# Gated product's sigmoids and roots left in PSUM, its squares on ScalarE

## The chip, the cores and the metric

The kernel runs on one core of one Trainium2 chip. The metric is the device time of one execution in microseconds. TensorE is called PE here, VectorE DVE, ScalarE ACT, GpSimd POOL and SyncE SP, as in the profile.

## The reference

The reference computes two blocks of a language model in fp32 over 1024 tokens (with 16 meta tokens before them) and a width of 1024. The first block mixes two branches, differential attention and a state-space model (SSM), each 512 wide. What the change touches is the end of the SSM branch. Its output `y` goes through

```python
y = jax.nn.gelu(y, approximate=False)
y = y * jax.nn.sigmoid(jnp.einsum('blc,cd->bld', y, w_glu[l]) + b_glu[l])
y = rms_norm(y, ssm_out_g[l]).astype(h.dtype)
mix = jnp.einsum('blc,cd->bld', jnp.concatenate([o, y], axis=-1), w_out[l])
```

where `o` is the attention's output. Behind it come a norm, a feed-forward of width 2816 and a second block with retention, a recurrent mixer and a feed-forward of its own.

## The kernel before, in words

Each engine has its own program, written as Python generators that are stepped in one common order. The 1024 tokens are worked in two halves of 512. A matrix product in nearly full fp32 is made of three products of split operands (high by high, low by high, high by low). Weights come in units of 128x1024, in a stream of fixed order (`ORDER`), into six slots. SP loads a unit into a slot when PE has released the unit six before it; POOL then splits it, first the high part (line 560), then the low part (line 562). PE's products with these units follow.

The gated product (`glu(h)` in the programs of ACT, PE and DVE) has features on the partitions: four tiles of 128x512, index `m`. It has six steps, and between them the stepping puts other work of the same engine.

- Steps 1 and 2: ACT issues 32 small loads of `y_raw`, applies Gelu in place and copies the high part `yh`. DVE makes the low part `yl`.
- Step 3: PE makes the products with the gate's weights, 48 matmuls (line 1752), into four PSUM banks: 2, 3, 0, 1 in half 0, and 4 to 7 in half 1.
- Step 4: ACT makes four sigmoids from PSUM into the SBUF tile `sig` (line 983) and loads the table of exp and ln. DVE multiplies `y_raw` by `sig` and squares it into `ysq`, tile by tile (lines 2572 and 2575). In half 0 it waits before the square for the second weight unit's products.
- Step 5: PE sums the squares over the 512 features with a matrix of ones (line 1759), in plain fp32, into the tile's first bank.
- Step 6: ACT makes the root `rinv` by ln and exp (lines 989 and 990) into SBUF. DVE scales `y_raw` by it and by the gain (line 2581), ACT copies the high part into `act_hi` (line 994), DVE makes the low part `act_lo` (line 2586).

ACT's operations have line 675 in the profile, DVE's `tt` line 2249 and `stt` line 2256, since helpers issue them. ACT's table loads have line 670.

What surrounds the two halves differs. In half 0 the steps 3 to 6 lie among the last steps of half 0's attention. ACT has that attention's last root (o_sq) between steps 4 and 6 and its last output copy ahead of step 6; DVE has the normalization o_n. After step 6, ACT stores the last query/key tile (line 808) and, when `glu_lo` has come, loads queries, keys and values of half 1's attention (lines 889 to 896). PE makes the first eight of the output product's 32 pieces (`mix_product(0)`, line 1854; one piece is six matmuls), then waits for the keys (line 1664). Those pieces use banks 0 to 3; bank 2 holds the sums of squares.

In half 1 the gated product is interleaved with half 0's feed-forward: behind step 3 stand 4 pieces of gate 20 (line 1813, six matmuls each), behind step 4 the 4 pieces of up 20, behind step 5 the 8 pieces of gate 21 and up 21, behind step 6 the last 16 pieces of the down product (line 1842). On DVE that puts the product `ff_f` (line 2930), its low part `ffh_lo` (line 2934) and the additions to `acc_dense` behind the steps; on ACT the silu `ff_f`, which needs another table, and the copy `ffh_hi`. A down piece waits until DVE has added the piece two before it. Then comes the norm of the feed-forward (`residual_half(0)`).

Of the kernel before, what the change touches and what calls it, by code (L numbers as in the profile page):

```python
# [7 lines left out]
F32, F32R, BF16 = mybir.dt.float32, mybir.dt.float32r, mybir.dt.bfloat16  # L8
ACT = mybir.ActivationFunctionType
ALU = mybir.AluOpType  # L10
X_AXIS = mybir.AxisListType.X
MUL, ADD, SUB = ALU.mult, ALU.add, ALU.subtract
# [51 lines left out]
class Tally:  # L64
# [11 lines left out]
    def give(self, ins, sem):  # L76

        self.eng.wait_ge(sem, self.post(ins, sem))
# [7 lines left out]
def build(nc, t):  # L86
# [179 lines left out]
    def glu_tiles(h):  # L266
        at = (ARENA, AT_MIX)[h]
        tiles_at = [place(f"y_raw_{h}", [P, 4, OCT, BANK // OCT], F32, at)]
        for n, (name, dt) in enumerate((("yh", F32R), ("yl", F32R), ("ysq", F32), ("sig", F32))):
            tiles_at.append(place(f"{name}_{h}", [P, 4, BANK], dt, at + 8192 * (n + 1 if h or n < 2 else 2 * n - 3)))  # L270
        tiles_at.append(place(f"rinv_{h}", [P, BANK], F32, at + (40960 if h else 16384)))
        return tiles_at

    glu_at = [glu_tiles(0), glu_tiles(1)]
# [383 lines left out]
    def _(act):  # L658
# [9 lines left out]
        def table_for(func):  # L668
            if loaded[0] != SETS[func]:
                act.preload_act_table_set(SETS[func])  # L670
                loaded[0] = SETS[func]

        def fn(out, in_, func, **kw):
            assert func not in SETS or loaded[0] == SETS[func]
            return act.activation(out, in_, func, **kw)  # L675
# [280 lines left out]
                    yield  # L956

        def glu(h):
            y_raw, yh, yl, ysq, sig, rinv = glu_at[h]
            if h == 0:  # L960
                spills_landed(0, 1)
            y_view = t["y_scratch"].rearrange("(t h) g c -> h t g c", h=SG)
            c0 = (META + BANK * h) // OCT
            for m in range(4):
                for j in range(8):
                    act.dma_start(y_raw[SG * j:SG * j + SG, m], y_view[:, :, 8 * m + j, c0:c0 + BANK // OCT]).then_inc(y_landed, 16)  # L966
            yield
            table_for(ACT.Gelu)
            act.wait_ge(y_landed, 16 * 32 * (h + 1))
            whole = lambda a, m: a[:, m].rearrange("p t c -> p (t c)")  # L970
            for m in range(4):
                give(fn(whole(y_raw, m), whole(y_raw, m), ACT.Gelu), act_step)
            for m in range(4):
                give(fn(yh[:, m], whole(y_raw, m), ACT.Copy), y_hi)
            yield
            yield
            table_for(ACT.Sigmoid)
            for m in range(4):
                if m % 2:
                    act.wait_ge(unit_done, AT[h, U_GLU + m // 2] + 1)  # L980
                else:
                    take(glu_psum)
                give(fn(sig[:, m], ps[:, glu_bank(h, m), :], ACT.Sigmoid, bias=glu_vec[:, m:m + 1]), glu_sig)
            table_for(ACT.Exp)
            yield
            yield
            table_for(ACT.Ln)
            take(glu_sum)
            give(fn(rinv[:, :], ps[:, glu_bank(h, 0), :], ACT.Ln, bias=eps_col, scale=1.0 / (4 * P)), act_step)
            give(fn(rinv[:, :], rinv[:, :], ACT.Exp, scale=-0.5), glu_root)  # L990
            cols = slice(META + BANK * h, META + BANK * h + BANK)
            for m in range(4):
                act.wait_ge(glu_prod, 4 * (2 * h + 1) + m + 1)
                give(fn(act_hi[:, 4 + m, cols].rearrange("p (c t) -> p t c", t=OCT), y_raw[:, m], ACT.Copy), glu_hi)
            yield
# [488 lines left out]
    def _(pe):  # L1484
# [250 lines left out]
                    yield  # L1735

        def glu(h):
            y_raw, yh, yl, ysq, sig, rinv = glu_at[h]
            yield
            yield  # L1740
            pe.wait_ge(y_lo, 4 * (h + 1))
            pe.wait_ge(*((o_lo, HEAD_UNITS * 2) if h else (y_kept, 2 * TB)))
            for m in range(4):
                pos = AT[h, U_GLU + m // 2]
                pe.wait_ge(w_ready, pos + 1)
                if h == 0 and m == 2:
                    pe.wait_ge(proj_kept, len(PROJ) + len(FAR))
                    pe.wait_ge(rope_done, ROPES + 8)
                for k in range(4):
                    w0 = BANK * (m % 2) + P * k  # L1750
                    for w, a in PASSES:
                        mm = pe.matmul(ps[:, glu_bank(h, m), :], ws[w][:, pos % SLOTS, w0:w0 + P], (yh, yl)[a][:, k, :],
                                       start=(k, w, a) == (0, 0, 0), stop=(k, w, a) == (3, 1, 0))
                post(mm, unit_done if m % 2 else glu_psum)
            yield
            yield
            for m in range(4):
                pe.wait_ge(glu_sq, 4 * h + m + 1)
                mm = pe.matmul(ps[:, glu_bank(h, 0), :], ones[:, :], ysq[:, m, :], start=m == 0, stop=m == 3)
            post(mm, glu_sum)  # L1760
            yield
            yield

        def mix_product(h):
            if h:
                pe.wait_ge(down_added, 2 * HALF * (FT // 2))
            else:
                pe.wait_ge(glu_sig, 4)
            for j, uu, k in OUT_ORDER:
                if (j, k) == (0, 0):  # L1770
                    pe.wait_ge(*((o_lo, HEAD_UNITS * (h + 1)) if uu < 2 else (glu_lo, 4 * (h + 1))))
                if j and uu == 0:
                    pe.wait_ge(mix_kept, 2 * HALF * h + k + 1)
                if (h, j, uu, k) == (0, 0, 0, 2):
                    pe.wait_ge(glu_root, 1)
                token_product(AT[h, U_OUT + 4 * j + uu], k, uu, acts, tok_cols(HALF * h + k), (0, 3, 0), mix_psum)
                yield

# [124 lines left out]
        def residual_half(h):  # L1903
            if h:
                pe.wait_ge(rw_norm, nth("norm", "out", NT - 1))
                pe.wait_ge(rw_act, nth("act", "y", NT - 1))
                pe.wait_ge(rw_dve, nth("dve", "st0", NT - 1))
            else:
                pe.wait_ge(glu_root, 2)
            tiles = tiles_of(2)[HALF * h:HALF * h + HALF]  # L1910
            for step in range(NORM_STEPS):
                if 1 <= step <= HALF:
                    g = tiles[step - 1][0]
                    pe.wait_ge(xn_ready, g + 1)
                    pe.wait_ge(act_ready, g - 1)
                    for k in range(KT):
                        mm = pe.transpose(ps[:, 4 + 2 * (g % 2) + k // 4, P * (k % 4):P * (k % 4) + P], xn_mix[:, g % 2, P * k:P * k + P], ident[:, :])
                    post(mm, turned)
                yield
            pe.wait_ge(act_ready, NT + 1 + HALF * (h + 1))  # L1920
# [323 lines left out]
    def _(dve):  # L2244
# [3 lines left out]
        def tt(out, a, b, op, signal=dve_step):  # L2248
            give(dve.tensor_tensor(out, a, b, op), signal)  # L2249
# [4 lines left out]
        def stt(out, a, s, b, op0, op1, signal=dve_step):  # L2254

            give(dve.scalar_tensor_tensor(out=out, in0=a, scalar=s, in1=b, op0=op0, op1=op1), signal)  # L2256
# [301 lines left out]
                yield  # L2558

        def glu(h):  # L2560
            y_raw, yh, yl, ysq, sig, rinv = glu_at[h]
            yield
            whole = lambda a, m: a[:, m].rearrange("p t c -> p (t c)")
            for m in range(4):
                take(y_hi)
                tt(yl[:, m], whole(y_raw, m), yh[:, m].bitcast(F32), SUB, y_lo)
            yield
            yield
            for m in range(4):
                take(glu_sig)  # L2570
                y = whole(y_raw, m)
                tt(y, y, sig[:, m], MUL, glu_prod)
                if h == 0:
                    dve.wait_ge(unit_done, AT[0, U_GLU + 1] + 1)
                tt(ysq[:, m], y, y, MUL, glu_sq)
            yield
            yield
            take(glu_root)
            for m in range(4):
                y = whole(y_raw, m)  # L2580
                stt(y, y, glu_vec[:, 4 + m:5 + m], rinv[:, :], MUL, MUL, glu_prod)
            cols = slice(META + BANK * h, META + BANK * h + BANK)
            for m in range(4):
                take(glu_hi)
                turned = lambda a: a[:, 4 + m, cols].rearrange("p (c t) -> p t c", t=OCT)
                tt(turned(act_lo), y_raw[:, m], turned(act_hi).bitcast(F32), SUB, glu_lo)
            yield
# [599 lines left out]
```

## Time and profile before

| | us |
|---|---|
| median of 3 runs | 3511.36 |
| lowest and highest | 3508.91, 3519.01 |
| profiled execution, its own time | 3521.95 |
| its span | 3520.0 |
| PE busy, of the span | 3117.6 |
| DVE busy | 1741.5 |
| ACT busy | 849.4 |
| POOL busy | 1975.2 |

All times in the trace are microseconds from the start of the span. The profiled execution is one of its own; none of the three runs was as long. A granted clock of 1.00 is PE's 2.4 GHz, 0.50 is 1.2 GHz. Matmuls overlap, so the time of one matmul in a row is longer than its distance to the next; for a train of matmuls the chain of waits gives the distance.

### The profile page before, as it was taken

The page shows a single profiled execution, that of the slowest core. Times are in us where ns is not written, and L with a number is a line of the kernel's source. Part 1 is how long each engine was busy: PE and PEld are TensorE (multiplying, and loading weights), DVE is VectorE, ACT ScalarE, POOL GpSimd, SP SyncE. Part 2 cuts the span into 40 slices and gives each one's busy share as a digit, 9 for nine tenths or more (in the row PEclk, how much of TensorE's full clock was granted, in tenths as well). Part 3 has the DMA queues.
Part 4 walks back from the last instruction along what each step waited for, and adds up shares of the span by engine and source line. Part 5 has one row for each costly group of instructions (what it writes and reads, how often), then busy time and mean ns, then how long its engine had stood idle before and what let it go on. Part 6 is the DMA issues. An engine that isn't in the chain of part 4 may idle for free.

```text
span 3520.0 us, 47870 instructions
## 1 busy us (share of the span) xinstructions
PE 3117.6 (89%) x19536; PEld 2399.0 (68%) x19536; DVE 1741.5 (49%) x2368; ACT 849.4 (24%) x1583; POOL 1975.2 (56%) x1076
## 2 busy tenths in 40 slices
PE   6997878799998749989999989988999988899997
PEld 4765546577776547767777767776777766688875
DVE  5844543444442641666655654376556564322233
ACT  3111122322221232122323223122222331200012
POOL 5710322454554545746666656665766674577873
PEclk9887888899999879999999999999999999899998
DMA  4343322222222324322222243432222222322231
GB/s 154 108 124 96 102 70 93 90 72 84 72 66 78 120 96 139 116 83 82 74 80 85 67 140 122 138 97 77 80 76 70 91 76 67 126 96 93 93 102 54
DMA packets 158027, 329.99 MB, mean 94 GB/s; under 512 B 34960, under 2 KB 74064, under 8 KB 157808
## 3 DMA queue, kind: packets, MB, share of 16 engines
q1 hardware_dynamic: 58752, 213.94, 19.2%
q10 hardware_dynamic: 99056, 112.99, 10.2%
q8 instruction: 155, 2.54, 0.3%
q14 instruction: 64, 0.52, 0.0%
HBM read 281.89 MB, written 44.97 MB: 93 GB/s over the span
## 4 chain that ended last, share of the span: by engine, by line
PE 72%; DVE 18%; ACT 3%; ACTq 3%; DMA 2%; issue 2%; POOL 0%; DVEq 0%
PE ps L1813 30%; PE ps L1854 12%; PE ps L1842 12%; PE ps L1664 2%; DVE acc_dense L2249 1%; DVE ffh_lo L2934 1%; DVE added L2249 1%; DVE cab_s L2249 1%; DVE act_lo L2249 1%; PE ps L1545 1%; PE ps L1585 1%; PE ps L2048 1%; ACTq L966 1%; DVE xn_dense L2256 1%; PE ps L1575 1%
## 5 line engine op out<-in xcount | busy, mean ns | idle before, releaser
L560 POOL TENSOR_TENSOR w_hi<-w_raw,ones 128x1024 fp32r<-128x1024 f32 x408 | 798.9, 1958 | 1268.5 <-DMA w_raw<-weights 1265.2
L562 POOL TENSOR_TENSOR w_lo<-w_raw,w_hi 128x1024 fp32r<-128x1024 f32 x408 | 1010.1, 2476 | 32.0
L1813 PE MATMUL ps<-act_hi,w_hi 128*128 128x512 f32 x1696 | 703.6, 415 | 13.6 <-ACT qk_raw L675 8.1
L1813 PE MATMUL ps<-act_lo,w_hi 128*128 128x512 f32 x1696 | 677.6, 400 | 0.0
L1813 PE MATMUL ps<-act_hi,w_lo 128*128 128x512 f32 x1696 | 673.4, 397 | 0.0
L1813 PEld LDWEIGHTS ps<-act_hi,w_hi 128*128 128x128 f32 x1696 | 323.6, 191 | 108.4 <-issue 16.5
L1813 PEld LDWEIGHTS ps<-act_hi,w_lo 128*128 128x128 f32 x1696 | 323.2, 191 | 74.9
L1813 PEld LDWEIGHTS ps<-act_lo,w_hi 128*128 128x128 f32 x1696 | 323.6, 191 | 67.1 <-issue 2.0
L2249 DVE TENSOR_TENSOR acc_dense<-acc_dense,ps 128x512 f32<-128x512 f32 x352 | 241.9, 687 | 232.2 <-PE ps L1842 173.3
L1842 PE MATMUL ps<-w_hi,ffh_hi 128*128 128x512 f32 x704 | 295.0, 419 | 56.3 <-DVE acc_dense L2249 55.0
L1842 PE MATMUL ps<-w_lo,ffh_hi 128*128 128x512 f32 x704 | 280.8, 399 | 0.0
L1842 PE MATMUL ps<-w_hi,ffh_lo 128*128 128x512 f32 x704 | 280.6, 399 | 0.0
L1854 PE MATMUL ps<-w_hi,act_hi 128*128 128x512 f32 x640 | 264.0, 412 | 14.8 <-issue 6.5
L1854 PE MATMUL ps<-w_hi,act_lo 128*128 128x512 f32 x640 | 258.8, 404 | 0.0
L1854 PE MATMUL ps<-w_lo,act_hi 128*128 128x512 f32 x640 | 257.5, 402 | 0.0
L2930 DVE TENSOR_TENSOR ff_f<-ff_f,ps 128x512 f32<-128x512 f32 x88 | 60.5, 688 | 374.5 <-PE ps L1813 373.7
L1842 PEld LDWEIGHTS ps<-w_hi,ffh_hi 128*128 128x128 f32 x704 | 135.5, 192 | 99.5 <-DVE acc_dense L2249 65.9
L670 ACT ACT_TABLE_LOAD x141 | 180.9, 1283 | 38.9 <-issue 29.4
L2337 DVE TENSOR_REDUCE small<-ps 128x1 f32<-128x144 f32 (+7 forms) x64 | 49.6, 774 | 223.4 <-PE ps L1666 223.2
L1854 PEld LDWEIGHTS ps<-w_hi,act_hi 128*128 128x128 f32 x640 | 125.1, 196 | 48.8 <-issue 12.3
L1842 PEld LDWEIGHTS ps<-w_lo,ffh_hi 128*128 128x128 f32 x704 | 135.4, 192 | 30.6
L1842 PEld LDWEIGHTS ps<-w_hi,ffh_lo 128*128 128x128 f32 x704 | 136.2, 193 | 25.3
(374 smaller groups left out, 4471.9 us busy)
## 6 DMA issues: line engine op xcount, KB each, us to landing
w_raw<-weights SPq DMA_DIRECT2D x408, 512.0 KB, 3.5
rw<-rw_t ACTq DMA_DIRECT2D x24, 256.0 KB, 2.5
rw<-lora_t ACTq DMA_DIRECT2D x24, 256.0 KB, 2.0
row<-x ACTq DMA_DIRECT2D x8, 512.0 KB, 3.8
row_dense<-x ACTq DMA_DIRECT2D x8, 512.0 KB, 4.1
res<-row_dense ACTq DMA_DIRECT2D x8, 512.0 KB, 2.6
row_mix<-res ACTq DMA_DIRECT2D x8, 512.0 KB, 7.6
res<-row_mix ACTq DMA_DIRECT2D x8, 512.0 KB, 2.8
```

Of the source, the lines that this page charges most:

```text
L560: pool.tensor_tensor(w_hi[:, s], raw, ones[:, 0:1].to_broadcast([P, 1024]), MUL).then_inc(w_hi_made, 1)
L562: pool.tensor_tensor(w_lo[:, s], raw, w_hi[:, s].bitcast(F32), SUB).then_inc(w_ready, 1)
L670: act.preload_act_table_set(SETS[func])
L966: act.dma_start(y_raw[SG * j:SG * j + SG, m], y_view[:, :, 8 * m + j, c0:c0 + BANK // OCT]).then_inc(y_landed, 16)
L1545: mm = pe.matmul(ps[:, n % 2, 0:c1 - c0], ws[w][:, pos % SLOTS, P * k:P * k + P], acts[a][:, k, c0:c1], start=(k, w, a) == (0, 0, 0), stop ...
L1664: mm = pe.matmul(out[:, c:c + w], q, k[:, META + c:META + c + w], start=True, stop=True)
L1813: mm = pe.matmul(out, ws[w][:, s, P * k:P * k + P], acts[a][:, k, x], start=(k, w, a) == (0, 0, 0), stop=(k, w, a) == (KT - 1, 1, 0))
L1842: mm = pe.matmul(ps[:, 2 + n % 2, :], ffh[a][:, m % 4, P * k:P * k + P], ws[w][:, s, BANK * j:BANK * j + BANK], start=(m % 2, w, a) == (0, ...
L1854: mm = pe.matmul(ps[:, kinds[2] + k, :], source[a][:, 2 * uu + kk, x], ws[w][:, pos % SLOTS, BANK * kk:BANK * kk + BANK], start=(uu, kk, w ...
L2249: give(dve.tensor_tensor(out, a, b, op), signal)
L2337: give(dve.tensor_reduce(small[:, col:col + 1], score_rows(h, u, br), X_AXIS, ALU.max, negate=True), s_max)
L2930: give(dve.tensor_tensor(ff_f[:, m % 2], ff_f[:, m % 2], ps[:, 1, :], MUL), ff_prod)
```

## The change

`sig` and `rinv` are no longer tiles in SBUF. The sigmoids go back into the PSUM banks that they are read from, and so does the root, in both of its steps. DVE reads both from PSUM. The squares are made by ACT, all four behind the table load of step 4, each after a wait for DVE's product; DVE's squares and its wait for the second unit are gone. Where PE waited for sigmoids or a root before it wrote to these banks again, it now waits for DVE's products: `glu_prod` counts eight in each half, four gated products and four scalings.

```diff
     def glu_tiles(h):
...
-        for n, (name, dt) in enumerate((("yh", F32R), ("yl", F32R), ("ysq", F32), ("sig", F32))):
+        for n, (name, dt) in enumerate((("yh", F32R), ("yl", F32R), ("ysq", F32))):
...
-        tiles_at.append(place(f"rinv_{h}", [P, BANK], F32, at + (40960 if h else 16384)))
...
 (ACT)   def glu(h):
...
-                give(fn(sig[:, m], ps[:, glu_bank(h, m), :], ACT.Sigmoid, bias=glu_vec[:, m:m + 1]), glu_sig)
+                give(fn(ps[:, glu_bank(h, m), :], ps[:, glu_bank(h, m), :], ACT.Sigmoid, bias=glu_vec[:, m:m + 1]), glu_sig)
             table_for(ACT.Exp)
+            for m in range(4):
+                act.wait_ge(glu_prod, 8 * h + m + 1)
+                give(fn(ysq[:, m], whole(y_raw, m), ACT.Square), glu_sq)
...
-            give(fn(rinv[:, :], ps[:, glu_bank(h, 0), :], ACT.Ln, bias=eps_col, scale=1.0 / (4 * P)), act_step)
-            give(fn(rinv[:, :], rinv[:, :], ACT.Exp, scale=-0.5), glu_root)
+            root = ps[:, glu_bank(h, 0), :]
+            give(fn(root, root, ACT.Ln, bias=eps_col, scale=1.0 / (4 * P)), act_step)
+            give(fn(root, root, ACT.Exp, scale=-0.5), glu_root)
...
 (PE)    def mix_product(h):
...
-                pe.wait_ge(glu_sig, 4)
+                pe.wait_ge(glu_prod, 4)
...
                 if (h, j, uu, k) == (0, 0, 0, 2):
-                    pe.wait_ge(glu_root, 1)
+                    pe.wait_ge(glu_prod, 8)
...
 (PE)    def residual_half(h):
...
-                pe.wait_ge(glu_root, 2)
+                pe.wait_ge(glu_prod, 16)
...
 (DVE)   def glu(h):
...
-                tt(y, y, sig[:, m], MUL, glu_prod)
-                if h == 0:
-                    dve.wait_ge(unit_done, AT[0, U_GLU + 1] + 1)
-                tt(ysq[:, m], y, y, MUL, glu_sq)
+                tt(y, y, ps[:, glu_bank(h, m), :], MUL, glu_prod)
...
-                stt(y, y, glu_vec[:, 4 + m:5 + m], rinv[:, :], MUL, MUL, glu_prod)
+                stt(y, y, glu_vec[:, 4 + m:5 + m], ps[:, glu_bank(h, 0), :], MUL, MUL, glu_prod)
```

## Rows read from the trace of the kernel before

**Rows 1.** The page: busy time by engine, and the chain that ended last.

```profile
PE 3117.6 (89%) x19536; PEld 2399.0 (68%) x19536; DVE 1741.5 (49%) x2368; ACT 849.4 (24%) x1583; POOL 1975.2 (56%) x1076
...
PE 72%; DVE 18%; ACT 3%; ACTq 3%; DMA 2%; issue 2%; POOL 0%; DVEq 0%
```

**Rows 2.** Chain in order of time, half 0: start, us, what.

```profile
540.97 2.40 DVE y_raw L2249
...
549.25 5.49 PE ps L1759 x6
...
555.35 0.70 ACT rinv L675
```

**Rows 3.** Chain in order of time, half 1.

```profile
1140.38 5.60 PE ps L1813 x24
...
1148.70 1.72 DVE y_raw L2249
...
1161.29 3.78 PE ps L1759 x4
1165.07 11.77 PE ps L1813 x48
...
1177.68 2.24 DVE y_raw L2256
...
1190.26 0.70 DVE acc_dense L2249
```

**Rows 4.** Tiles y_raw, acc_dense, rw_t: duration ns min/median/max, first and last start.

```profile
L2249 DVE TENSOR_TENSOR y_raw<-y_raw,sig x8: 691/2018/2717, 541.0 to 1161.3; 128x512 f32<-128x512 f32 x8
L2249 DVE TENSOR_TENSOR ysq<-y_raw x8: 691/693/2711, 543.4 to 1162.0; 128x512 f32<-128x512 f32 x8
L2256 DVE SCALAR_TENSOR_TENSOR y_raw<-y_raw,small,rinv x8: 751/752/2724, 556.8 to 1183.0; 128x512 f32<-128x512 f32 x8
...
L2249 DVE TENSOR_TENSOR act_lo<-y_raw,act_hi x8: 1078/1141/1290, 560.0 to 1189.1; 128x512 fp32r<-128x512 f32 x8
...
L2249 DVE TENSOR_TENSOR acc_dense<-acc_dense,ps x352: 686/687/692, 765.5 to 3427.4; 128x512 f32<-128x512 f32 x176
...
L2256 DVE SCALAR_TENSOR_TENSOR rw_t<-ps,rw_vec_s,rw_t x28: 749/749/751, 1329.5 to 2242.8; 128x511 f32<-128x511 f32 x28
```

**Rows 5.** Timeline of POOL, 1174 to 1186: start, us, engine, line, what.

```profile
1174.99 1.89 POOL L560 TENSOR_TENSOR w_hi<-w_raw,ones 128x1024 fp32r<-128x1024 f32 x1 [15.03 <-DMA w_raw<-weights]
1176.97 2.40 POOL L562 TENSOR_TENSOR w_lo<-w_raw,w_hi 128x1024 fp32r<-128x1024 f32 x1
1180.41 2.04 POOL L560 TENSOR_TENSOR w_hi<-w_raw,ones 128x1024 fp32r<-128x1024 f32 x1 [1.05 <-DMA w_raw<-weights]
1182.53 2.68 POOL L562 TENSOR_TENSOR w_lo<-w_raw,w_hi 128x1024 fp32r<-128x1024 f32 x1
```

**Rows 6.** Timeline of DVE, half 1, the low parts.

```profile
1185.79 4.43 DVE L2249 TENSOR_TENSOR act_lo<-y_raw,act_hi 128x512 fp32r<-128x512 f32 x4
```

**Rows 7.** Timelines of ACT, the table loads behind the sigmoids.

```profile
541.25 1.28 ACT L670 ACT_TABLE_LOAD   x1
...
1150.78 1.28 ACT L670 ACT_TABLE_LOAD   x1
```

**Rows 8.** Groups of ACT by form: busy us, mean ns, idle before.

```profile
L675 ACT ACTIVATE yh<-y_raw 128x512 fp32r<-128x512 f32 x8 | 5.1, 632 | 0.3
```

**Rows 9.** Windows: us, busy time by engine, granted clock, DMA share.

```profile
544.00:545.00 1.00, 0.86 (x2) 0.30 (x2) 0.97 (x2) 0.00 (x0) 1.00 (x1) 1.00 0.00 0
...
546.00:547.00 1.00, 0.00 (x0) 0.00 (x0) 0.96 (x2) 0.00 (x0) 1.00 (x1) 0.50 0.00 0
```

**Rows 10.** Waits of PE, 526 to 582: us, times, longest.

```profile
PE ps L1664 <- DMA k_pair<-qk_scratch: 8.0, 1, 8.0
```

**Rows 11.** Timeline of PE, start of the output product.

```profile
555.81 0.47 PE L1854 MATMUL ps<-w_hi,act_hi 128*128 128x512 f32 x1 [0.87 <-issue]
```

**Rows 12.** Tile acc_dense, the residual additions: min/median/max ns.

```profile
L2249 DVE TENSOR_TENSOR row_mix<-row_mix,acc_dense x8: 1224/2012/3253, 1217.1 to 2105.1; 128x1024 f32<-128x1024 f32 x8
```

More of the change, by code:

```diff
@@ L958, in glu @@
         def glu(h):
-            y_raw, yh, yl, ysq, sig, rinv = glu_at[h]
+            y_raw, yh, yl, ysq = glu_at[h]
             if h == 0:
@@ L1737, in glu @@
         def glu(h):
-            y_raw, yh, yl, ysq, sig, rinv = glu_at[h]
+            y_raw, yh, yl, ysq = glu_at[h]
             yield
@@ L2560, in glu @@
         def glu(h):
-            y_raw, yh, yl, ysq, sig, rinv = glu_at[h]
+            y_raw, yh, yl, ysq = glu_at[h]
             yield
```

## The prediction, made before the changed kernel ran

> **What bounds the kernel now.** The page comes first: TensorE (PE) is busy for 89% of the span, and 72% of the chain that ended last is PE's, 18% VectorE's (DVE) [rows 1]. So time is to be had only where the chain leaves PE. The chain by time shows two such places in the changed code. In half 0 it runs on DVE from 540.97, the first product of y and sigmoid, to the last sums of squares, and reaches the logarithm of the root at 555.35 [rows 2]. In half 1 it is on DVE from 1148.70 to 1161.29, on PE to 1176.84, and on DVE again from 1177.68 to 1190.95, when PE goes on with the feed-forward [rows 3]. The end of the half-0 stage leads into the load of K, for which PE waits 8.0 us [rows 10].
>
> The forms of the tiles say why DVE is slow there. Its instructions with both tensors in SBUF take 0.69 or 0.75 us at best and 2.7 us at worst: y times sigmoid has a median of 2.02 us. The same operations with one operand in PSUM take 0.686 to 0.692 us in all 352 cases, and 0.749 to 0.751 us in all 28 [rows 4]. The long ones lie beside GpSimd's (POOL's) splits of weights, which take about 1.9 and 2.4 us alone and 2.04 and 2.68 us where DVE is in the way [rows 5]. The two exclude each other when DVE reads two SBUF tensors, and a PSUM operand takes DVE out of it.
>
> **The change, part by part, half 0.** Products: each goes from up to 2.7 us to 0.69 us. Four with 0.03 us between, from 540.97, end at 543.87. DVE's four squares are gone. Squares: ACT (ScalarE) does them at 0.63 us, the size of its copy between SBUF tiles [rows 8], after the table load that ends at 542.53 [rows 7]; the first product is done by 541.7. They end at 543.2, 543.9, 544.5 and 545.2. Behind them on ACT wait the attention's last root (three small instructions, done by about 546.2) and DVE's normalization behind it, just in time for PE's turn of the output. Sums: the last three took 5.49 us at the lower clock (0.50 granted) [rows 2, 9], 1.83 us each, so 0.92 at the full clock. Before, the clock was still full in 544 to 545 and at 0.50 in 546 to 547, after some three microseconds in which PE had done little but the first sum [rows 9]. Now the four sums follow each other from 543.25, so I take the full clock: 3.66 us, end 546.9. The old tail from the sums to the logarithm is 555.35 less 554.74, 0.61 us; the new logarithm starts at 547.5. **Gain 7.85 us.**
>
> What follows keeps its length: root, scalings from PSUM at 0.75 us as now, ACT's copies, the stores, the loads. The new wait of the output product's third tile, for all four scalings instead of the root, stops PE. PE starts that product at 555.81 [rows 11]; two tiles of six matmuls (5.60/24 each [rows 3]) last 2.8 us, to 558.6; the scalings end 3.1 us after the root, at 559.9. PE stands 1.3 us, with everything queued behind it. That costs nothing, since PE then waits 8.0 us for K anyway [rows 10]; 6.7 us of the cover are left. Without that cover it would cost the 1.3 us. The weight slot of this product also comes free 1.3 us later; the next split then lies behind DVE's low parts, not among them. The residual's new wait, for 16 products instead of root 2, is over before PE comes to it, more than 20 us later.
>
> **Half 1.** The sigmoids start as now, the products end at 1151.6. ACT's table load ends at 1152.06 [rows 7], so the first square is there at 1152.7 and the last at 1154.7. Behind them on ACT wait the feed-forward's high part and a table load; DVE's low part needs them, PE not before the products 18 us later. The sums run from 1152.75 to 1156.4; before, PE went on from them at 1165.07. The next 48 matmuls took 11.77 us, partly at the lower clock; at twice 5.60 for 24 they take 11.2 [rows 3]. They end at 1167.6 instead of 1176.84: 9.2 us.
>
> Then the DVE stretch, counted from its first scaling (1177.68 before). Before, scalings and low parts took 12.55 us, the low parts 4.43 of them without a meeting [rows 6]. Four scalings from PSUM now take 3.1 us, 5 us less. But POOL's next split follows PE's release of a slot, so it keeps its distance: 2.73 us after the first scaling (1180.41) [rows 5]. The low parts read two SBUF tensors (y and its high part) and come at 3.1 us, into that split. They wait until 4.6; the first (1.08 us) ends at 5.7; POOL's second instruction, 2.4 us, gets in next, to 8.1; the other three end at 11.4. What the scalings win comes back to 1.2 us. **Gain 9.2 + 1.2 = 10.4 us.**
>
> Bounds of what no row shows. ACT writing PSUM: at the lower end nothing changes (0.69 us); at the far end twice that. It would add 0.7 us for the last sigmoid and 1.3 for the root in half 0, and 2.8 for four sigmoids in half 1: 4.8 us. I take the lower end, because DVE's own accesses to PSUM are no slower [rows 4]. A product reading PSUM is bounded by 0.687 and by 2.7; 380 rows lie at the lower end [rows 4]. The removed tiles and the removed wait of DVE for the second unit (long done) cost and give nothing.
>
> Squares moved to ACT cost 0.63 us against 0.69 on DVE [rows 8, 4]. The Trainium skill, page "ScalarE: Activation LUTs", section "Rules for kernel authors", says that such plain arithmetic belongs on VectorE; by the rows of fp32 here the move would lose nothing per instruction. The page "VectorE: DVE Perf Modes", section on the TRN2 errata, gives a PSUM source 62 cycles more than an SBUF source; as an estimate that is 0.065 us, and for some eight instructions on the path 0.5 us less gain. The rows show no such difference.
>
> **Sum:** 7.85 + 10.4 = 18.25 us. The profiled execution took 3521.95 us (span 3520.0), so it would become 3503.7. It lies 10.6 us above the median of the three runs (3511.36, 3508.91 to 3519.01), a difference spread over a program whose other parts the change leaves alone, so I take the sum off the median: **3493.1 us**.
>
> **Rivals.**
> *The meeting does not move.* If POOL's split comes later than the low parts, these keep 4.43 us and the DVE stretch wins 4.95 instead of 1.2: 3489.3 us. For it: only 0.4 us decide (2.73 against 3.1). Against it: if DVE goes first, POOL's work falls between its instructions all the same. Chance 0.13.
> *The clock stays low.* If the sums in both halves run at 0.50, each set takes 3.66 us more and the matmuls behind them 0.6: 7.9 us of the gain are gone, 3501.0 us. For it: the fall before 546 came soon after short work, and short work precedes the sums now too. Against it: the gaps that preceded the fall are filled. Chance 0.17.
> *PSUM writes are slow, or small losses add up,* so that under 10.5 us are left: about 3502 to 3509. Chance 0.12.
> *Lost meetings behind the stage: slower.* The norms after 1213 read two SBUF tensors, 1024 wide, and lie on the chain. The residual additions take 1.22 us at least, 2.01 in the median and 3.25 at most [rows 12]: a lost meeting with POOL costs up to 2.0 us. Between 1213 and 1320 there are 24 instructions of this kind. Nine new losses use up the gain, and from fifteen on the kernel is slower by more than can be told: 18.25 less 30 is 11.7 us more, 3523 us. Against it: many of the 24 are lost already, and POOL's splits and DVE's norms both follow PE's releases and shift together. Chance 0.03.
>
> **How the numbers follow.** The forecast case has 0.55, at 3493, with 4 us each way for the runs' own spread. A measurement of this kernel tells some 0.3%, 10.5 us, from no change. The range takes in the case without the meeting below (3489, less 5 for the spread) and the low clock above (3501, plus 4): 3484 to 3505. Faster: the forecast and the first rival, nearly all, plus some of the low-clock case, which lies at the edge: 0.79. Same: the rest of that and the small losses, 0.17. Slower: 0.04.
>
> **What would show it.** Products and scalings at 0.69 and 0.75 us, all sixteen; squares on ACT at 0.63; sums in one train, 3.4 to 3.7 us, at a granted clock of 1.00; the half-0 logarithm 6.5 us after DVE's first product instead of 14.4; PE's stop of 1.3 us before the third output tile, with the wait for K shorter by as much; in half 1 the low parts at 2 us or more for the first two, and PE resuming about 10.4 us sooner, net of the shift from half 0. I am wrong if products from PSUM are long beside POOL, if the sums have 1.7 us each, if the K wait grows by what the stage lost, or if the norms after the stage take longer than before.

## The result, and the profile after

| us | median | lowest, highest | runs | ratio to before |
|---|---|---|---|---|
| before, measured beside it | 3519.2 | 3508.91, 3522.39 | 6 | |
| changed kernel | 3493.7 | 3486.75, 3499.16 | 6 | 0.9933 [0.9915, 0.9952] |
| its profiled execution | 3495.0 | | 1 | (span 3492.8) |

The ratio gives 0.67% less time, about 24 us, with an interval from 17 to 30 us; the two medians are 25.5 us apart. So the changed kernel is faster, clear of the noise. The prediction was 3493.1 us.

Runs of one and the same kernel lie 13 us apart in the table above (kernel before), and up to 34 us in a longer series (act_squares, below). Spans differ too: a second trace of the kernel before has 3506.9 us where the first has 3520.0. So two spans cannot show terms of a few microseconds. What can be compared is a short stretch between two named instructions, and the readings of terms below are such stretches.

The chain by time of the changed kernel shows half 0. Columns as in [rows 2].

```profile
530.84 1.21 ACT L669
...
532.14 0.64 ACT ysq L674
...
532.82 3.70 PE ps L1762 x8
...
537.03 0.67 ACT ps L674
...
544.30 2.21 DMA qk_scratch<-qk_raw
...
548.25 5.79 DMA k_pair<-qk_scratch
...
554.08 2.50 PE ps L1667 x4
```

DVE has left the chain between the sigmoids and the logarithm. What stands there is ACT's last sigmoid, its table load, one square, and one train of sums. DVE's first product started at 530.59, the logarithm at 537.03: 6.44 us, where [rows 2] have 14.38. The same chain in half 1:

```profile
1130.22 0.64 ACT ysq L674
...
1130.90 3.70 PE ps L1762 x8
1134.60 11.16 PE ps L1816 x48
...
1146.60 0.76 DVE y_raw L2259
...
1149.73 2.48 DVE act_lo L2252
...
1152.23 3.13 DVE act_lo L2252
...
1155.38 1.09 DVE act_lo L2252
...
1156.49 1.09 DVE act_lo L2252
...
1157.61 0.70 DVE acc_dense L2252
1158.35 11.78 PE ps L1845 x41
```

The view of the tiles `y_raw` and `ysq` (min, median and max in ns, as in [rows 4]) shows that not one of the 24 instructions moved to PSUM or to ACT is long any more; only the low parts, which still read two tensors in SBUF, are:

```profile
L2252 DVE TENSOR_TENSOR y_raw<-y_raw,ps x8: 686/686/689, 530.6 to 1129.1; 128x512 f32<-128x512 f32 x8
L674 ACT ACTIVATE ysq<-y_raw x8: 629/630/632, 532.1 to 1132.2; 128x512 f32<-128x512 f32 x8
L2259 DVE SCALAR_TENSOR_TENSOR y_raw<-y_raw,small,ps x8: 747/748/748, 538.4 to 1149.0; 128x512 f32<-128x512 f32 x8
L2252 DVE TENSOR_TENSOR act_lo<-y_raw,act_hi x8: 1078/1220/3115, 541.5 to 1156.5; 128x512 fp32r<-128x512 f32 x8
```

On the timeline of ACT are two operations whose price no row of before had, a sigmoid and the root's exponential written to PSUM:

```profile
530.16 0.66 ACT L674 ACTIVATE ps<-ps,small 128x512 f32<-128x512 f32 x1 [2.06 <-PE ps L1755]
...
537.73 0.58 ACT L674 ACTIVATE ps<-ps 128x512 f32<-128x512 f32 x1
```

The last view is PE's waits over the half-0 stage (us, times, longest). The new stall is there, 1.0 us, but the wait for the keys has gone from 8.0 us [rows 10] to 3.9. That is 4.1 us less, four times what the stall explains:

```profile
PE ps L1667 <- DMA k_pair<-qk_scratch: 3.9, 1, 3.9
PE ps L1857 <- DVE y_raw L2259: 1.0, 1, 1.0
```

Three stretches carry the change. The first runs from DVE's first product of half 0 to the logarithm; the second from there to the first matmul on the keys; the third from DVE's first product of half 1 to PE's next down piece. "Store" and "unit" are when, after the logarithm, ACT issues the store `qk_scratch<-qk_raw` and SP the next 512 KB weight unit. The rows below `after_again` (a second trace of the changed kernel) are the experiments described below.

| us | to log | to keys | half 1 | store | unit |
|---|---|---|---|---|---|
| before | 14.38 | 19.84 | 42.30 | 7.45 | 6.28 |
| before_again | 13.62 | 20.28 | 42.11 | 7.45 | 6.28 |
| changed | 6.44 | 17.05 | 31.43 | 7.26 | 7.61 |
| after_again | 6.44 | 17.19 | 31.60 | 7.27 | 7.61 |
| psum_products | 12.53 | 19.91 | 35.42 | 7.46 | 6.28 |
| act_squares | 11.71 | 17.63 | 36.09 | 7.43 | 7.91 |
| psum_root | 13.56 | 17.42 | 39.84 | 7.24 | 7.60 |
| stall_alone | 14.42 | 17.01 | 42.48 | 7.37 | 7.70 |
| no_stall | 6.44 | 19.45 | 31.24 | 7.38 | 6.28 |
| low_through_psum | 6.44 | 17.07 | 28.07 | | |
| late_sums | 9.92 | 17.34 | 33.29 | | |
| stall_all | 6.44 | 17.26 | 31.39 | 6.93 | 11.78 |
| early_keys | 6.38 | 13.07 | 31.28 | | |
| early_and_low | 6.38 | 13.07 | 28.08 | | |

Before to changed, the three gave 7.94, 2.79 and 10.87 us, 21.6 together. The spans differ by 27.2: another 10.4 us lie ahead of the first product, and 5.9 were given back between the first square of the norm that follows half 1's stage and the end. Both are in code that the change leaves alone. The remaining 1.1 us lie between the stretches. The second trace of before starts its first product at 528.68 (first trace 540.97, changed 530.59), so the 10.4 are not the change's.

### The profile page after: what moved, and what is told of

Its sections match the earlier page's. It is cut to its first block, busy times and chain, and to the rows that moved or that the text cites. A ratio compares the mean times of both kernels' runs of the same rounds, so it can differ in the third digit from the quotient of the medians.

```text
span 3492.8 us, 47873 instructions
## 1 busy us (share of the span) xinstructions
PE 3110.7 (89%) x19536; PEld 2397.2 (69%) x19536; DVE 1719.1 (49%) x2360; ACT 854.1 (24%) x1591; POOL 1974.2 (57%) x1076
## 4 chain that ended last, share of the span: by engine, by line
PE 75%; DVE 15%; ACT 3%; ACTq 3%; issue 2%; DMA 2%; POOL 0%; DVEq 0%
PE ps L1816 31%; PE ps L1845 12%; PE ps L1857 12%; PE ps L1667 2%; PE ps L1578 2%; DVE acc_dense L2252 1%; PE ps L1548 1%; DVE act_lo L2252 1%; DVE ffh_lo L2934 1%; PE ps L2051 1%; DVE added L2252 1%; ACTq L965 1%; PE ps L1588 1%; DVE xn_dense L2259 1%; PE ps L1695 1%
## 5 line engine op out<-in xcount | busy, mean ns | idle before, releaser
L1857 PE MATMUL ps<-w_hi,act_hi 128*128 128x512 f32 x640 | 263.7, 412 | 15.3 <-issue 6.5
L1845 PEld LDWEIGHTS ps<-w_hi,ffh_lo 128*128 128x128 f32 x704 | 136.9, 194 | 25.5
```

What stands on the lines that cost most here:

```text
L1845: mm = pe.matmul(ps[:, 2 + n % 2, :], ffh[a][:, m % 4, P * k:P * k + P], ws[w][:, s, BANK * j:BANK * j + BANK], start=(m % 2, w, a) == (0, ...
L1857: mm = pe.matmul(ps[:, kinds[2] + k, :], source[a][:, 2 * uu + kk, x], ws[w][:, pos % SLOTS, BANK * kk:BANK * kk + BANK], start=(uu, kk, w ...
```

## Experiments: the parts one by one

There are two theories of the gain. By the first, it comes from meetings. A meeting is a DVE instruction with both tensors in SBUF that falls beside one of GpSimd's splits: the two shut each other out, and what frees DVE is an operand in PSUM. By the rival theory, it is the count of DVE's instructions in the stage that matters. Each part was put alone on the kernel before, beside that kernel itself.

```diff
 psum_products
-give(fn(sig[:, m], ps[:, glu_bank(h, m), :], ACT.Sigmoid, ...), glu_sig)
+give(fn(ps[:, glu_bank(h, m), :], ps[:, glu_bank(h, m), :], ACT.Sigmoid, ...), glu_sig)
...
-pe.wait_ge(glu_sig, 4)
+pe.wait_ge(glu_prod, 4)
...
-tt(y, y, sig[:, m], MUL, glu_prod)
+tt(y, y, ps[:, glu_bank(h, m), :], MUL, glu_prod)
 act_squares
+for m in range(4):
+    act.wait_ge(glu_prod, 8 * h + m + 1)
+    give(fn(ysq[:, m], whole(y_raw, m), ACT.Square), glu_sq)
...
-if h == 0:
-    dve.wait_ge(unit_done, AT[0, U_GLU + 1] + 1)
-tt(ysq[:, m], y, y, MUL, glu_sq)
 psum_root
-give(fn(rinv[:, :], ps[:, glu_bank(h, 0), :], ACT.Ln, ...), act_step)
-give(fn(rinv[:, :], rinv[:, :], ACT.Exp, scale=-0.5), glu_root)
+root = ps[:, glu_bank(h, 0), :]
+give(fn(root, root, ACT.Ln, ...), act_step)
+give(fn(root, root, ACT.Exp, scale=-0.5), glu_root)
...
-pe.wait_ge(glu_root, 1)
+pe.wait_ge(glu_prod, 8)
...
-pe.wait_ge(glu_root, 2)
+pe.wait_ge(glu_prod, 16)
...
-stt(y, y, glu_vec[:, 4 + m:5 + m], rinv[:, :], MUL, MUL, glu_prod)
+stt(y, y, glu_vec[:, 4 + m:5 + m], ps[:, glu_bank(h, 0), :], MUL, MUL, glu_prod)
```

> The kernel before, unchanged, for a second trace. If the 10.7 us by which the changed kernel's trace is ahead before it reaches the gated product have nothing to do with the change, this trace lies anywhere up to 11 us ahead of the first one at that point (first gelu at 503 to 514 us), while from the first gated product to the first logarithm it again takes 14.4 us, and from the first scaling to the end of the low parts in half 1 12.5 us. If they come from the change, this trace again has its first gelu at 514 us.

Measured: 3508.9 us in one run, span 3506.9. This says how finely the rest can be read: the same program a second time differs by 13.1 us in the span, and by 0.8, 0.4 and 0.2 us in the three stretches.

> Only the sigmoids stay in PSUM; the squares stay on VectorE between the products, the root in SBUF. Theory of the meetings: products 0.69 us, squares (two reads of one SBUF tile) still up to 2.7 us. From the first product to the last square 9.8 us in half 0 instead of 11.1, and 9.5 instead of 14.0 in half 1; the sums still run at half clock in part. Gain 6 us in all, range 4 to 8. Rival (the products' meetings were all of it): squares all at 0.69, 5.8 us from first product to last square in both halves, gain 13 us or more.

Measured: 3507.64 us, ratio 0.9992 [0.9975, 1.0009] over 12 runs. The tile view:

```profile
L2249 DVE TENSOR_TENSOR y_raw<-y_raw,ps x8: 686/686/687, 528.0 to 1139.9; 128x512 f32<-128x512 f32 x8
L2249 DVE TENSOR_TENSOR ysq<-y_raw x8: 691/1566/2257, 528.7 to 1140.6; 128x512 f32<-128x512 f32 x8
```

All products are short, and the squares, whose median was 0.69 us [rows 4], are now long: they inherit the meetings. 1.1 to 1.9 us are won in half 0 and 6.8 in half 1, together at or just above the upper end of the 4 to 8 us expected.

> Only the squares go to ScalarE; sigmoids and root stay in SBUF. Theory of the meetings: the products keep their long ones, beside GpSimd (first to last product end 8.5 us in half 0, 9 us in half 1); the squares follow 0.7 us behind. Gain 2.8 + 4.2 = 7 us, range 5 to 9. Rival (the number of VectorE's instructions counts, not where they read): as the changed kernel up to the root, gain 15 us or more.

Measured: 3503.7 us, ratio 0.9982 [0.9963, 1.0001] over 12 runs. The tile view has the mirror image:

```profile
L2252 DVE TENSOR_TENSOR y_raw<-y_raw,sig x8: 693/2266/2720, 527.0 to 1135.5; 128x512 f32<-128x512 f32 x8
L675 ACT ACTIVATE ysq<-y_raw x8: 629/629/631, 529.5 to 1137.9; 128x512 f32<-128x512 f32 x8
```

Four instructions fewer per half, and the products that are left are longer than before (median 2.27 against 2.02 us). 1.9 to 2.7 us are won in half 0, 6.1 in half 1. So the count of instructions is not what matters.

> Only the root stays in PSUM, with the new wait of the output product's third piece. Theory: the scalings of half 1 take 3.1 us instead of 8.1, but the low parts behind them then meet GpSimd, so 1.6 us are left there. In half 0 the stage itself keeps its length; TensorE's stall of 1 us makes the next weight unit start behind the store of the last query/key tile, which then lands in 2.2 us instead of 4.2, and the load of K is earlier by 2 to 3 us. Gain 3.5 to 4.5 us. Rival (the stall only costs, or is hidden): the store lands in 4.2 us again and the gain is 1.5 us.

Measured: 3515.59 us, ratio 1.0002 [0.9983, 1.002] over 12 runs. 2.4 us are won in half 1, and 0.1 to 0.8 us up to half 0's logarithm, which is no more than two traces of one program differ; "to keys" is 2.4 to 2.9 us shorter. Its timeline of DVE shows the scalings' gain going to the low parts, which took 4.43 us [rows 6]:

```profile
1161.20 3.10 DVE L2257 SCALAR_TENSOR_TENSOR y_raw<-y_raw,small,ps 128x512 f32<-128x512 f32 x4
1164.34 7.96 DVE L2250 TENSOR_TENSOR act_lo<-y_raw,act_hi 128x512 fp32r<-128x512 f32 x4
```

What follows: in half 1 the parts alone give 6.8 + 6.1 + 2.4 = 15.3 us, together 10.9: products and squares remove partly the same meetings. In half 0 it is the other way round: 1.1 to 1.9 and 1.9 to 2.7 alone, 7.2 to 7.9 together. Only the pair takes the stretch off DVE altogether, and only with the pair do the sums run as one train at a granted clock of 1.00; in the parts alone the mean over the sums was 0.67 (psum_products) and 0.86 (act_squares). How much of the surplus each of the two gives was not separated. The three kernels with 12 runs each also show what a median can't tell here: they are worth 5 to 11 us in the stretches, and not one of their ratios is clear of 1.

But the table has something that neither theory had: two of these kernels have the shorter way to the keys, and psum_products has not. In psum_root the new wait stalls PE. act_squares has no such wait. Its windows show PE's output product starting at a granted clock of 0.50, while in psum_products it started at 541 with the clock at 1.00:

```profile
539.00:540.00 1.00, 0.87 (x2) 0.80 (x3) 0.03 (x1) 0.97 (x2) 0.00 (x0) 0.50 0.00 0
540.00:541.00 1.00, 1.00 (x4) 0.71 (x4) 0.84 (x2) 0.05 (x2) 0.00 (x0) 0.50 0.00 0
```

In psum_root and act_squares alike, PE gives up its weight slot later after the logarithm, and the next unit goes out at 7.60 and 7.91 us instead of 6.28.

## Experiments: the stall that was costed at nothing

The theory formed from the table: what decides "to keys" is the order of two transfers. The weight unit goes out when PE has freed its slot. Where that is before ACT's store of half 0's keys, the store shares the DMA engines with 512 KB; where PE was held up for about a microsecond, by a wait or by a low clock, the store goes first. The rivals: the keys came sooner by chance, or through faster work on ACT. (The keys' load waits for two things, the store's landing and DVE's low parts.)

> The changed kernel, unchanged, timed in the same job as the versions beside it. The stage's own stretches repeat: first product to first logarithm 6.4 us in half 0 (14.4 before), logarithm to K 17.1 (19.8), first product to the feed-forward's resumption 31.4 in half 1 (42.3). If what follows the stage varies by chance only, the time is 19 to 24 us under the kernel before. If meetings lost behind the stage take part of it back, as single traces hint (2312 to 2316 us from there to the end in three changed kernels, 2303 to 2306 in two traces of the kernel before and one other), it is 13 to 18 us under it.

Measured: 3491.15 us (3490.03 to 3495.84), ratio 0.993 [0.9914, 0.9947] over 5 runs. All three stretches are within 0.2 us of the first trace's.

```diff
 stall_alone, on the kernel before
-pe.wait_ge(glu_root, 1)
+pe.wait_ge(glu_prod, 8)
 no_stall, on the changed kernel: half 0's root in SBUF again, and its wait
-give(fn(root, root, ACT.Exp, scale=-0.5), glu_root)
+give(fn(root if h else rinv_0[:, :], root, ACT.Exp, scale=-0.5), glu_root)
...
-pe.wait_ge(glu_prod, 8)
+pe.wait_ge(glu_root, 1)
...
-stt(y, y, glu_vec[:, 4 + m:5 + m], ps[:, glu_bank(h, 0), :], MUL, MUL, glu_prod)
+stt(y, y, glu_vec[:, 4 + m:5 + m], ps[:, glu_bank(h, 0), :] if h else rinv_0[:, :], MUL, MUL, glu_prod)
```

> The kernel before with one changed wait: the output product's third piece waits for all four scalings. Theory that the stall reorders two transfers: TensorE stands 1 to 1.3 us, the next weight unit is requested after the store of the last query/key tile (7.6 against 7.45 us behind the logarithm, instead of 6.3), the store lands in 2.2 us instead of 4.2, and K's product comes 17.4 to 17.9 us behind the logarithm instead of 19.8 to 20.3: 2.5 us gained by a wait. Rival (the shorter way to K in the changed kernel is chance): 19.8 to 20.3 again, no gain.

Measured: 3510.75 us, ratio 0.9985 [0.9968, 1.0001] over 10 runs. PE stalls for 1.1 us and the keys come 2.8 us sooner; the other two stretches stay as they were. DVE's low parts end 9.59 us after the logarithm (9.63 before), so faster work ahead of the loads is not the reason. The chain by time, first of the kernel before:

```profile
562.80 4.15 DMA qk_scratch<-qk_raw
...
568.37 6.77 DMA k_pair<-qk_scratch
...
575.19 2.50 PE ps L1664 x4
```

and of stall_alone:

```profile
556.64 2.20 DMA qk_scratch<-qk_raw
...
560.40 5.85 DMA k_pair<-qk_scratch
...
566.29 2.50 PE ps L1664 x4
```

The order can be read off the timelines of the two queues. The kernel before has the weight unit 1.17 us ahead of the store:

```profile
561.63 0.33 SPq L547 DMA_DIRECT2D w_raw<-weights  x1
...
562.80 0.33 ACTq L808 DMA_DIRECT2D qk_scratch<-qk_raw  x1
```

The changed kernel has the store 0.34 us ahead:

```profile
544.30 0.33 ACTq L807 DMA_DIRECT2D qk_scratch<-qk_raw  x1
...
544.64 0.33 SPq L546 DMA_DIRECT2D w_raw<-weights  x1
```

> The changed kernel, but half 0's root goes to SBUF in its second step and the output product waits for the root alone, so TensorE does not stand. Theory: weight unit ahead of the store again, logarithm to K 19.8 to 20.4 us instead of 17.1, while first product to logarithm stays 6.4; 2.8 us more than the changed kernel. Rival: 17 us, as in the changed kernel.

Measured: 3493.06 us, ratio 0.9938 [0.9918, 0.9959] over 4 runs. "To keys" is back at 19.45 us and the unit at 6.28, with "to log" unchanged: taking the stall away costs 2.4 us. Store and keys took 3.10 and 7.51 us in its chain. So it is shown from both sides that the wait brings the keys sooner, by adding it to the one kernel and by removing it from the other.

The traces hold a second exchange, which the theory above did not have. SP issues one more weight unit 5.57 us behind the first (5.58 in stall_all), and it moves along. In the kernel before it goes out ahead of the second of the two loads of keys, in the changed kernel behind it (two lines of the kernel before, then two of the changed one):

```profile
567.20 0.33 SPq L547 DMA_DIRECT2D w_raw<-weights  x1
568.37 0.80 ACTq L890 DMA_DIRECT2D k_pair<-qk_scratch  x1
...
548.25 0.45 ACTq L889 DMA_DIRECT2D k_pair<-qk_scratch  x1
550.21 0.33 SPq L546 DMA_DIRECT2D w_raw<-weights  x1
```

This unit was out 0.01 to 1.2 us ahead of that load in before, before_again, psum_products and no_stall, and the load took 6.8 to 8.3 us; in the other ten traces it went out behind it, and the load took 5.8 to 6.3. The store took 3.0 to 4.15 us in the first four and 2.0 to 2.2 in the others. How the gain divides between the two exchanges was not separated, and it varies: the store gave 1.9 us and the load 1.0 against the first trace of before, 0.8 and 2.5 against the second. In the changed kernel the store has nothing more to give: it lands 9.47 us after the logarithm, and DVE's low parts, for which the loads wait too, end at 9.51.

```diff
 stall_all, on the changed kernel
-pe.wait_ge(glu_prod, 4)
+pe.wait_ge(glu_prod, 8)
```

> The changed kernel, but the whole output product waits for the four scalings, not its third piece alone: TensorE stands about 3.5 us at its head. Theory of the cover: TensorE waits for K 4.3 us anyway, so logarithm to K stays 17.0 to 17.4 us and the idle time ahead of K shrinks to about 1.5 us (or 1.0); the weight unit is requested 3 us later still and lies wholly behind the store. Rival (the cover is used up, or the weight unit now meets K's load): logarithm to K grows by 1 us or more.

Measured: 3494.48 us in one run. All of PE's pieces now wait for the scalings. In its waits the stall is 4.9 us, where 3.5 were expected, and no wait for the keys is left:

```profile
PE ps L1857 <- DVE y_raw L2259: 4.9, 1, 4.9
```

"To keys" is 17.26 us, against 17.05 and 17.19 in the changed kernel: 3.9 us more of stall were paid by the wait for the keys. That a stall here is covered was right, but with this one the cover is used up. PE came last, not the keys: they landed 16.66 us after the logarithm. After its pause PE ran the start of the output product at a granted clock of 0.50, and the product's 48 matmuls took 12.8 us instead of 11.2. The unit, now 4.9 us behind the store, let the keys land only 0.35 to 0.5 us sooner than one 0.3 us behind it; the loads were waiting for the low parts (9.24 us), not for the store (landed at 8.94).

## Experiments: what is left in the stage

```diff
 low_through_psum, on the changed kernel, half 1 (banks in the order 1, 2, 3, 0)
-stt(y, y, glu_vec[:, 4 + m:5 + m], ps[:, glu_bank(h, 0), :], MUL, MUL, glu_prod)
+stt(ps[:, glu_bank(h, m), :] if h else y, y, glu_vec[:, 4 + m:5 + m], ps[:, glu_bank(h, 0), :], MUL, MUL, glu_prod)
...
-tt(turned(act_lo), y_raw[:, m], turned(act_hi).bitcast(F32), SUB, glu_lo)
+scaled = ps[:, glu_bank(h, m), :].rearrange("p (t c) -> p t c", t=OCT) if h else y_raw[:, m]
+tt(turned(act_lo), scaled, turned(act_hi).bitcast(F32), SUB, glu_lo)
```

ACT copies half 1's high part from the same PSUM banks, and PE's wait behind the stage is for the low parts instead of the products.

> The changed kernel, with half 1's scaled products written to their PSUM banks, from where ScalarE copies the high part and VectorE makes the low part with one SBUF and one PSUM operand. Theory of the meetings: the four low parts take 4.4 us instead of 7.8, though GpSimd's split lies on them; first product to resumption 28.0 us instead of 31.4; 3.4 us gained. Rival (the low parts are long for another reason, as their strided writes): 7.8 us again, no gain.

Measured: 3491.58 us, ratio 0.9929 [0.9909, 0.9949] over 6 runs. Half 1's stretch is 28.07 us. Its timelines of DVE and GpSimd show the low parts in the same place beside a split, and neither is longer for it:

```profile
1148.43 4.45 DVE L2253 TENSOR_TENSOR act_lo<-ps,act_hi 128x512 fp32r<-128x512 f32 x4
...
1147.98 1.89 POOL L559 TENSOR_TENSOR w_hi<-w_raw,ones 128x1024 fp32r<-128x1024 f32 x1 [1.27 <-DMA w_raw<-weights]
1149.95 2.37 POOL L561 TENSOR_TENSOR w_lo<-w_raw,w_hi 128x1024 fp32r<-128x1024 f32 x1
```

In the changed kernel they took 7.84 us beside splits of 1.89 and 3.07. One operand in PSUM is what ends a meeting, here as in the products.

```diff
 late_sums, on the changed kernel
-pe.wait_ge(glu_sq, 4 * h + m + 1)
+pe.wait_ge(glu_sq, 4 * h + 4)
```

> The changed kernel, but TensorE starts each half's sums when all four squares are there: 2.0 us later, after a gap of 2.6 us in half 0 and 3.1 in half 1. Theory (it matters that the sums follow the work ahead of them at once): in at least one half the granted clock is at 0.50 in the sums, which then take up to 7.4 us instead of 3.7, and first product to first logarithm in half 0 is 10 to 12 us instead of 6.4. Rival (the clock holds over such a gap): sums 3.7 us in both, first product to logarithm 8.4 us, first product to resumption 33.5 instead of 31.5.

Measured: 3502.73 us in one run. In half 0 the first sum starts 4.21 us after the first product instead of 2.23, and the eight matmuls take 5.19 us instead of 3.70. The windows of half 0 (columns as in [rows 9]) show why:

```profile
537.00:538.00 1.00, 0.00 (x0) 0.00 (x0) 0.14 (x1) 0.94 (x3) 0.63 (x1) 1.00 0.00 0
538.00:539.00 1.00, 0.51 (x1) 0.50 (x2) 0.00 (x0) 0.94 (x4) 1.00 (x1) 0.56 0.03 8
539.00:540.00 1.00, 1.00 (x2) 0.34 (x1) 0.35 (x1) 0.37 (x2) 0.92 (x2) 0.50 0.00 0
...
541.00:542.00 1.00, 1.00 (x3) 0.53 (x2) 0.00 (x0) 0.00 (x0) 0.68 (x1) 0.73 0.00 0
542.00:543.00 1.00, 1.00 (x3) 0.38 (x2) 0.00 (x0) 0.00 (x0) 0.00 (x0) 1.00 0.00 0
```

PE had stood still for some 2.6 us, and the granted clock went to 0.50 (1.2 GHz) under the sums. In half 1 it stood for 3.1 us, but the clock stayed at 1.00 and the sums took 3.70 us; there only the delay was lost, 1.9 us. PE had done short matmuls of the attention before the pause in half 0, full trains in half 1; whether that makes the difference is not shown by one trace. So the low-clock rival was a real danger in half 0, though smaller than the theory of this run had it (9.92 us to the logarithm, where it said 10 to 12): one run puts its price there at 1.5 us, besides the delay itself.

```diff
 early_keys, on the changed kernel, half 0
-store_far(7)
...
-for r in range(2):
-    act.wait_ge(qk_stored[r], 16 * 8)
-load_queries_and_keys(1, 0)
...
+if h == 0:
+    store_far(7)
...
+if h == 0:
+    for r in range(2):
+        act.wait_ge(qk_stored[r], 16 * 8)
+    load_queries_and_keys(1, 0)
```

The store moves from behind the high parts to behind the squares, the loads from behind the low parts to behind the root's exponential.

> The changed kernel, with the last query/key tile stored ahead of the logarithm and Q and K of the next attention loaded between the root and ScalarE's four high parts. Theory (what is left of the wait for K is the store and the load behind the high parts): K lands before TensorE is through with its eight pieces, logarithm to K 12.7 to 13.5 us instead of 17.1, 3.5 to 4.5 us gained; the low parts come 2.1 us later and delay nobody. Rival (the loads take ScalarE's time and the low parts, 2 us later, hold up the output product's next pieces): the gain is 2 us or less.

Measured: 3497.36 us, ratio 0.9944 [0.9923, 0.9965] over 5 runs. Its timeline of ACT shows the keys' path ahead of the scalings:

```profile
537.07 0.33 ACTq L806 DMA_DIRECT2D qk_scratch<-qk_raw  x1
...
539.97 0.46 ACTq L888 DMA_DIRECT2D k_pair<-qk_scratch  x1
```

"To keys" is 13.07 us, 4.0 less, and PE no longer waits for them.

> Both together: Q and K early, and half 1's low parts through PSUM. They lie in different halves, so they should add: logarithm to K 13 us, first product to resumption in half 1 28.0 us, 7.5 us under the changed kernel, some 29 us (0.8%) under the kernel before. Rival (a meeting or a wait behind takes one of them back): no faster than the low parts through PSUM alone.

Measured: 3491.68 us, ratio 0.9928 [0.9905, 0.995] over 6 runs. The stretches add up, 13.07 and 28.08 us: 7.3 to 7.6 less than in the two traces of the changed kernel. But its ratio can't be told from the changed kernel's 0.9933 and 0.993, nor can those of the two parts; the median of early_keys is even the highest of the four. That this version beats the changed kernel is read in the stretches of one trace, and is not shown in time.

## Why the prediction was right, and the step in it that was wrong

The time, the sign and the range held. Step by step:

- **Half 0, 7.85 us.** Measured 7.94. Products at 0.69 us, squares at 0.63, sums as one train at the granted clock of 1.00 and 3.70 us long (taken as 3.66), the logarithm at 6.44 us (taken as 6.5).
- **Half 1 up to the end of the 48 matmuls, 9.2 us.** Measured from the first product: 28.14 us before, 18.84 after, 9.3 gained. The 48 matmuls took 11.16 us, as twice 5.60 said.
- **The DVE stretch of half 1, 1.2 us.** Measured 1.57 (12.54 before, 10.97 after, from the first scaling). GpSimd's split came 2.76 us after the first scaling, where 2.73 was worked out, so the meeting moved as predicted; it was just less dear, 7.84 us for four low parts instead of 8.3. The first rival, that the low parts keep 4.43 us, failed by 0.35 us of distance, and low_through_psum shows that 3.4 of its 3.75 us were really there to be had.
- **ACT's writes to PSUM, bounded by 0.69 and twice that.** They are at the lower end and slightly below: 0.66 us against 0.69 for the sigmoid, 0.58 against 0.63 for the root's exponential. The Trainium skill, page "ScalarE: Activation LUTs", section "Step-by-step: what each stage is for", calls PSUM the destination with less latency for this engine; the traces agree, by 0.03 us for the sigmoid and 0.02 us for the exponential. (In no_stall the exponential from PSUM to SBUF took 0.60 us, so the rest of its 0.05 us comes with the source.)
- **DVE's reads of PSUM.** The 62 cycles more that the Trainium skill, page "VectorE: DVE Perf Modes", section on the TRN2 errata, gives a PSUM source are not seen: 0.686 us with an operand in PSUM, 0.691 without.
- **Lost meetings behind the stage.** They did not come. The residual additions, 2.01 us in the median in both traces of before [rows 12], have 1.23 in both traces of the changed kernel; but three variants that contain the change (late_sums, early_keys, early_and_low) have 2.01 again, so this is not a sure gain of the change. From PE's resumption to the first square of the norm that follows it took 22.51 us against 22.98.
- **The step that failed: the stall of 1.3 us, "that costs nothing".** It measured 1.0 us, and its cover was there, as stall_all shows. But a delay costed at nothing also moves what hangs on it. The prediction itself had the slot free 1.3 us later, and used it for GpSimd's next split only. There was nothing to move there: in the kernel before that split starts 9.83 us after the logarithm, and the low parts have ended at 9.63. It did not put that slot's weight unit, and the one after it, beside ACT's store and the keys' load on the DMA engines. The unit was 1.17 us ahead of the store and came to lie 0.34 us behind it, and the next unit came to lie behind the keys' load: the store took 2.21 us instead of 4.15 (3.04 in before_again), the keys' load 5.79 instead of 6.77 (8.33), and "to keys" came down by 2.79 us. Of the 21.6 us in the stretches, 18.8 are the predicted sum of 18.25, and the rest is this.

The profiled execution's 10.6 us above the median were put down to the spread and not to the stage: before_again agrees, with a span 13.1 us shorter and each stretch of the stage as long to within 0.8 us. The sum was off by 3.3 us against the stretches, less than the runs of one kernel differ. But that the forecast of 3493.1 us came within 0.6 us of the measured time is luck. The sum of 18.25 us was taken off 3511.36, the median of three runs; beside the changed kernel the kernel before had 3519.2 over six runs, from which the same sum gives 3501. The measured gain of 24 us, with its interval from 17 to 30, fits the 21.6 us of the stretches and the 18.25 forecast alike.

The rule of the Trainium skill, page "ScalarE: Activation LUTs", section "Rules for kernel authors", that puts such products on VectorE would have kept the meetings. By the rows a square on ACT is 0.06 us shorter, and six of the eight squares left on DVE in psum_products took 1.5 to 2.3 us. The Trainium skill, page "SBUF — State Buffer", section "Who interferes with whom", calls the port pair that DVE and GpSimd share an exclusive lock. The traces agree: in psum_products a square of 0.69 us took up to 2.26 beside a split, and in low_through_psum the low parts went from 7.84 to 4.45 us with one operand in PSUM.

## What to carry to other kernels

Where DVE and GpSimd work side by side on SBUF tensors, look for operands that already lie in PSUM and leave them there, and look which instruction inherits the meeting: in half 0 either part alone was worth 1 to 3 us, the pair 7 to 8. When a stall is costed at nothing because a later wait covers it, list every transfer and release behind it and set their new times against those of the other queues; here a shift by 1.3 us that exchanged their order was worth 2.4 to 2.8. And where runs of one kernel spread by 20 us and more, settle terms of a few microseconds in stretches between named instructions, and prove them by adding and removing the one wait.

## What the runs showed that was not expected

- A 256 KB store took 3.0 to 3.1 us in three traces (before_again, psum_products, no_stall) and 4.15 in one (before) when issued 1.1 to 1.2 us behind a 512 KB load on another queue, and 2.2 us when issued 0.3 us ahead of it. Both traces of the kernel before have it 1.17 us behind, so the distance does not make the difference between 3.0 and 4.15; what does stays open.
- A stall of PE made the kernel's stage shorter: 2.8 us gained for 1.1 us of waiting (stall_alone), 2.4 us lost for removing it (no_stall). Both are read in single traces; in time neither kernel can be told from the one that it was made from.
- A pause of PE of 2.6 us was followed by a granted clock of 0.50 in half 0, while one of 3.1 us left it at 1.00 in half 1 (late_sums, one trace).
- Code that the change leaves alone took between 2302.5 and 2316.0 us from the first square of the norm behind half 1's stage to the end, over 14 traces. The two traces of before have 2306.0 and 2303.9, the two of the changed kernel 2311.9 and 2305.7; so few traces show no relation to the variant. Where this comes from was not tried.
